# Six ring places up to the 78th gather, the second tile's projection and norm over slots 40 to 81, late modulation rows behind the attention output

## What is computed

```python
mod = silu(c) @ w_ada + b_ada                      # sh1 sc1 g1 sh2 sc2 g2, 6 x 1024
h = x * (1 + sc1) + sh1
qa, ka, va, qb, kb, vb = split(h @ w_in)           # 1024 x 3072
ya = rms_norm(moba_attention(qa, ka, va)); yb = rms_norm(dilated_attention(qb, kb, vb))
y = concat([ya, yb]) @ w_out
x = layer_norm(ALPHA * x + (1 + g1) * y, ln1_g, ln1_b)
h2 = x * (1 + sc2) + sh2
# peer_ffn: 8 heads; product keys pick 16 of 16384 experts for each token and head
s1, s2 = scores of q = h2 @ w_q_peer against sub_keys   # top 16 of each, top 16 of the sums -> e, g
f = sum over the 128 picked experts of gelu(h2 . u[e]) * g * v[e]
x = layer_norm(ALPHA * x + (1 + g2) * f, ln2_g, ln2_b)
```

## Time and profile before

| what | us |
|---|---|
| median of 3 runs | 816.12 (815.91 to 816.32) |
| the profiled execution | 814.11 |
| its span in the trace | 812.3 |
| PE busy | 683.8 |
| VectorE busy | 581.1 |
| ScalarE busy | 346.0 |
| POOL busy | 291.3 |
| DMA | 323.74 MB, mean 399 GB/s |

### The profile page before, as it was taken

One profiled execution on the slowest core, in us unless ns is written; L12 is line 12 of the kernel. 1 busy time (PEld: TensorE's weight loads), 2 busy tenths in 40 slices (PEclk: granted clock), 3 DMA queues, 4 the chain that ended last, 5 costly groups with the idle time before them and its releaser, 6 DMA issues.

```text
span 812.3 us, 7319 instructions
## 1 busy us (share of the span) xinstructions
PE 683.8 (84%) x1988; PEld 325.7 (40%) x1988; DVE 581.1 (72%) x1349; ACT 346.0 (43%) x994; POOL 291.3 (36%) x263
## 2 busy tenths in 40 slices
PE   8999978998999898787989777787878787877785
PEld 4887644554544364443333223222323222222221
DVE  5566968787777987777777878767676757675455
ACT  0013322685575644353545355434343535353333
POOL 1000000344444365554454433443434343434340
PEclk9999999999999999997979999999999999999999
DMA  9999995899999999999999999999999999999993
GB/s 301 379 402 413 416 419 200 356 349 420 392 395 419 422 421 420 421 422 421 420 422 422 419 422 422 420 421 422 422 422 420 422 422 421 422 421 422 421 411 137
DMA packets 57213, 323.74 MB, mean 399 GB/s; under 512 B 6162, under 2 KB 16722, under 8 KB 20946
## 3 DMA queue, kind: packets, MB, share of 16 engines
q0 software_dynamic: 37152, 268.45, 80.0%
q1 hardware_dynamic: 19138, 54.55, 17.5%
q10 hardware_dynamic: 882, 0.27, 0.2%
HBM read 322.18 MB, written 1.07 MB: 398 GB/s over the span
## 4 chain that ended last, share of the span: by engine, by line
DMA 55%; PE 23%; DVE 9%; ACT 6%; issue 4%; SPq 1%; POOL 1%; DVEq 0%; ACTq 0%
DMA ring<-in_experts,e_all 51%; PE bank L529 12%; PE bank L551 4%; DVE ring L882 4%; DMA QT_h2T<-in_w 2%; DMA ring<-in_w 2%; PE bank L601 2%; PE bank L518 2%; ACT diag L728 2%; DVE acc L1038 1%; ACT weight L719 1%; POOL ring L1203 1%; SPq L402 1%; ACT L715 1%; ACT gel L715 1%
## 5 line engine op out<-in xcount | busy, mean ns | idle before, releaser
L529 PE MATMUL bank<-ring,diag 128*128 128x512 f32 x956 | 473.1, 631 | 104.5 <-ACT diag L728 104.3
L1203 POOL DMA_INDIRECT ring<-in_experts,e_all x254 | 282.8, 1113 | 495.1 <-PE bank L529 301.5
L529 PEld LDWEIGHTS bank<-ring,diag 128*128 128x128 f32 x956 | 173.2, 196 | 380.7 <-ACT diag L728 225.8
L882 DVE CUSTOM_DVE_ANT_0 ring<-ring,T_h 128x1024 f32<-128x1024 f32 x128 | 156.7, 1225 | 109.1 <-DMA ring<-in_experts,e_all 109.1
L882 DVE CUSTOM_DVE_ANT_0 ring<-ring,h 128x1024 f32<-128x1024 f32 x128 | 156.6, 1224 | 63.7 <-DMA ring<-in_experts,e_all 61.2
L715 ACT ACTIVATE gel<-pre 128x1 f32<-128x1 f32 x256 | 51.8, 202 | 313.3 <-DVE pre L882 312.5
L728 ACT ACTIVATE diag<-consts,weight 128x128 f32<-128x128 f32 x239 | 95.9, 401 | 7.8
L719 ACT ACTIVATE weight<-gel,g_all 128x1 f32<-128x1 f32 x256 | 75.4, 295 | 9.3
L1038 DVE SCALAR_TENSOR_TENSOR acc<-ring,cact,acc 128x512 f32<-128x512 f32 x56 | 42.1, 752 | 5.4 <-DMA ring<-in_w 3.0
L551 PE MATMUL bank<-hT_yT,lnw 128*128 128x256 f32 x128 | 28.7, 380 | 0.9 <-DVE hT_yT L1003 0.9
L601 PE MATMUL bank<-ring,hT_yT 128*128 128x512 f32 x64 | 28.5, 596 | 0.7 <-DMA ring<-in_w 0.7
(11 more groups left out here) (195 smaller groups left out, 572.9 us busy)
## 6 DMA issues: line engine op xcount, KB each, us to landing
ring<-in_w SPq DMA_DIRECT2D x16, 1024.0 KB, 14.2
H_s<-in_w SPq DMA_DIRECT2D x7, 1024.0 KB, 10.1
ring<-in_w SPq DMA_DIRECT2D x12, 512.0 KB, 10.5
ring<-in_w SPq DMA_DIRECT2D x16, 256.0 KB, 6.5
lnw<-in_w SPq DMA_DIRECT2D x4, 1024.0 KB, 17.7
ring<-in_experts,e_all POOLq DMA_INDIRECT x254, 14.8
H_s<-in_w SPq DMA_DIRECT2D x5, 512.0 KB, 8.2
lnw<-in_w SPq DMA_DIRECT2D x4, 512.0 KB, 8.4
```

The lines of the kernel that those rows point to most:

```text
L529: last = nc.tensor.matmul(tile_sum(t)[n], diag[:, m % DIAGS, :], ring[:, RING_AT[i], D + CH * n:D + CH * n + CH], start=(s == 0), stop=(s ...
L882: nc.vector.tensor_tensor_reduce(ring[:, r, 0:D], ring[:, r, 0:D], h2[i // SLOTS], 1.0, 0.0, ALU.mult, ALU.add, pre[:, i % PAIR:i % PAIR + ...
L1203: nc.gpsimd.indirect_dma_start(ring[:, r, :], None, A["experts"], bass.IndirectOffsetOnAxis(ap=e_all[:, i:i + 1], axis=0)).then_inc(slot_i ...
```

## The change

`WIDE_FROM` goes from 42 to 78, so gathers 42 to 77 use six places. In `PLAN` the first two rows of chunk 10 (`wsuma`, 10, 0) stand behind `yT` (0, 1) and `wo` (0, 0, 1) and no longer ahead of `PV` 2 and 3. `BESIDE` is written anew: nothing but the copy of v is left at slot 0, the units of S come in pairs at 2, 10, 19 and 27, `wo` at 40, 41, 49 and 52, `xa` at 52, `ln1a` at 56, `ln1b` at 67, `hT` at 70, the queries of tile 1 at 72 to 81. Slots 38 and 45 are added by VectorE. Slot 11 comes two places behind its dot. `ln1b` writes `h2` in two halves, and each transpose waits for its own half.

```diff
--- before.py
+++ after.py
@@ -80,7 +80,7 @@
 
 NARROW = [0, 1, 6, 7, 4, 5]
 WIDE = [2, 3] + NARROW
-WIDE_FROM = 42
+WIDE_FROM = 78
 
 
 G1, SH2, SC2, G2 = range(4)
@@ -100,8 +100,8 @@
        ("wsum", 4), ("S", 0), ("S", 1), ("v", 0, 0), ("wsum", 5), ("qk", 2, 0), ("qk", 2, 1), ("Tr", 0), ("Tr", 1), ("PV", 0), ("PV", 1), ("modrow", 0), ("madd", 0),
        ("yT", 0, 0), ("wsum", 6), ("qk", 3, 0), ("modrow", 1), ("madd", 1), ("wsum", 7),
        ("qk", 3, 1), ("modrow", 2), ("madd", 2), ("wsum", 8), ("S", 2), ("S", 3), ("modrow", 3), ("madd", 3), ("wsum", 9), ("v", 1, 0),
-       ("modrow", 4), ("madd", 4), ("Tr", 2), ("Tr", 3), ("wsuma", 11), ("wo", 0, 0, 0), ("wsuma", 10, 0), ("PV", 2), ("PV", 3), ("ny", 0), ("modrow", 5), ("madd", 5),
-       ("yT", 0, 1), ("wo", 0, 0, 1), ("xa", 0), ("wsuma", 10, 1), ("wo", 0, 1, 0), ("rows2",), ("wo", 0, 1, 1), ("ln1a", 0),
+       ("modrow", 4), ("madd", 4), ("Tr", 2), ("Tr", 3), ("wsuma", 11), ("wo", 0, 0, 0), ("PV", 2), ("PV", 3), ("ny", 0), ("modrow", 5), ("madd", 5),
+       ("yT", 0, 1), ("wo", 0, 0, 1), ("wsuma", 10, 0), ("xa", 0), ("wsuma", 10, 1), ("wo", 0, 1, 0), ("rows2",), ("wo", 0, 1, 1), ("ln1a", 0),
        ("va", 1, 1), ("ln1b", 0), ("hT", 0, 0), ("hT", 0, 1), ("wsumb", 10), ("wsumb", 11), ("q", 0, 0),
        ("s", 0, 0, 0), ("s", 0, 0, 1), ("v", 1, 1), ("modrow", 6), ("madd", 6), ("modrow", 7)]
     + [("piece", 0, 0), ("early",), ("q", 0, 1)] + [("piece", 0, j) for j in range(1, EXP_PIECE)] + [("v", 0, 1)]
@@ -110,18 +110,18 @@
 
 HEAD1 = [(1,), (2, 3), (4,), (5, 6), (7,), (8,), (9, 10), (11,)]
 LAG = 2
-NARROW_LAG, NARROW_TO = 1, 12
+NARROW_LAG, NARROW_TO = 1, 11
 VA_STEPS = 6
 
-BY_DVE = [20, 22, 35, 36, 37] + [i for i in range(48, 112) if i % 16 in (2, 4, 5)]
+BY_DVE = [20, 22, 35, 36, 37, 38, 45] + [i for i in range(48, 112) if i % 16 in (2, 4, 5)]
 FOLD = 114
 BESIDE = {
-    0: [("vcopy", 0, 1), ("S", 4), ("S", 5), ("Tr", 4)], 2: [("PV", 4), ("Tr", 5)], 3: [("s", 0, 1, 0), ("s", 0, 1, 1)], 5: [("PV", 5)],
-    6: [("S", 6), ("S", 7)], 8: [("Tr", 6), ("Tr", 7)], 12: [("PV", 6)], 15: [("PV", 7), ("S", 8)], 17: [("S", 9)], 19: [("yT", 1, 1), ("Tr", 8)],
-    20: [("Tr", 9)], 23: [("PV", 8)], 25: [("PV", 9), ("S", 10), ("S", 11)], 27: [("q", 0, 2)], 28: [("Tr", 10)], 29: [("s", 0, 2, 0)], 32: [("Tr", 11)],
-    34: [("PV", 10), ("s", 0, 2, 1)], 36: [("PV", 11)], 37: [("ny", 1), ("yT", 1, 0)], 38: [("wo", 1, 1, 0), ("wo", 1, 0, 0)],
-    40: [("wo", 1, 1, 1), ("wo", 1, 0, 1), ("xa", 1)], 44: [("ln1a", 1)], 47: [("ln1b", 1)], 50: [("hT", 1, 0), ("hT", 1, 1)], 52: [("q", 1, 2)],
-    56: [("q", 0, 3)], 60: [("q", 1, 3)], 66: [("s", 0, 3, 0)], 68: [("q", 1, 0)], 70: [("s", 0, 3, 1)], 76: [("q", 1, 1)], 116: [("x1", 0)], 119: [("x1", 1)],
+    0: [("vcopy", 0, 1)], 2: [("S", 4), ("S", 5)], 3: [("Tr", 4)], 4: [("s", 0, 1, 0)], 5: [("s", 0, 1, 1)], 6: [("PV", 4), ("Tr", 5)],
+    10: [("PV", 5), ("S", 6), ("S", 7)], 13: [("Tr", 6), ("Tr", 7)], 16: [("PV", 6), ("PV", 7)], 19: [("S", 8), ("S", 9)], 21: [("yT", 1, 1), ("Tr", 8)],
+    22: [("Tr", 9)], 23: [("PV", 8)], 25: [("PV", 9)], 27: [("S", 10), ("S", 11)], 30: [("q", 0, 2)], 32: [("Tr", 10), ("s", 0, 2, 0)], 34: [("Tr", 11)],
+    35: [("PV", 10), ("PV", 11), ("ny", 1)], 38: [("yT", 1, 0)], 39: [("s", 0, 2, 1)], 40: [("wo", 1, 1, 0)], 41: [("wo", 1, 0, 0)], 43: [("q", 0, 3)],
+    49: [("wo", 1, 1, 1)], 52: [("wo", 1, 0, 1), ("xa", 1)], 56: [("ln1a", 1)], 66: [("s", 0, 3, 0)], 67: [("ln1b", 1)], 68: [("s", 0, 3, 1)],
+    70: [("hT", 1, 0), ("hT", 1, 1)], 72: [("q", 1, 2)], 75: [("q", 1, 3)], 78: [("q", 1, 0)], 81: [("q", 1, 1)], 116: [("x1", 0)], 119: [("x1", 1)],
 } | {84 + 2 * i + z: [("s", 1, i, z)] for i in range(4) for z in range(2)} | {96 + 2 * j: [("lnb", j // 2, j % 2)] for j in range(8)}
 
 
@@ -658,7 +658,7 @@
                     product(dst[:], lambda k: yT[t][:, KC // 2 * g + k, :], lambda k: w[:, KC // 2 * g + k, :], KC // 2).then_inc(full, 1)
                 elif kind == "hT":
                     t, i = step[1:]
-                    pe.wait_ge(h2_ready, t + 1)
+                    pe.wait_ge(h2_ready, 2 * t + i + 1)
                     for j in range(4):
                         last = nc.tensor.transpose(dst[:, P * j:P * j + P], h2[t][:, P * (4 * i + j):P * (4 * i + j) + P], ident)
                     last.then_inc(full, 1)
@@ -1120,8 +1120,10 @@
                     dve.wait_ge(rows2_ready, 1)
                     centre(t, x[:, t, :], mod[:, SC2, :], h2[t])
                     inverse(t)
-                    scale(t, h2[t], mod[:, SH2, :], h2[t]).then_inc(h2_ready, 1)
-                    dve.wait_ge(h2_ready, t + 1)
+                    for n in range(2):
+                        half = slice(CH * n, CH * n + CH)
+                        scale(t, h2[t][:, half], mod[:, SH2, half], h2[t][:, half]).then_inc(h2_ready, 1)
+                    dve.wait_ge(h2_ready, 2 * t + 2)
                 elif kind == "x1":
                     t = step[1]
                     filled(dve, ("PV", len(UNITS) - 1))
```

## The result

The changed kernel takes 822.61 us (median of 4 runs, 819.28 to 823.61) against 816.01 beside it (815.03 to 816.32): the ratio is 1.0079, interval 1.0051 to 1.0108, so it is slower by 6.6 us. The profiled execution is its fastest: 819.28 us with a span of 817.4, 5.1 more than the span before. What follows explains these 5.1 us; the 2 to 4 us by which the other runs are longer are in no trace.

What follows compares the result with a forecast made beforehand. The DMA's ceiling of about 420 GB/s bounds the kernel, so only its losses can change. Head -3.2, ring 1.3 + 4.7 = 6.0 against 7.5, so -1.5; together -4.7, from 816.12 to 811.4 us, range 806.3 to 816.5.

Steps and rivals of the forecast that it cites:

- The head: Way to the first gather: rows2 starts 2.9 us earlier, at ln1's landing, h2's halves give 0.3; 3.2 us gained.
- the 0.5 that was worked out: h2 in two halves in the head: PE starts its transposes 0.55 us earlier; 0.3 us was taken for the product.
- The start of the ring: Slot 0 right behind v(0,1): gather 6 at 153.0, and the 4.8 us lost there go but for about 0.5.
- up to slot 41: Ring from its start to slot 41: 1.3 us of loss in all, bounds 0.3 and 4, start's 0.5 included.
- Slots 42 to 77: Stretch now with six places: bursts of work bring holds over the limit; 4.7 us lost, bounds 0.5 and 13.
- limit of 8.7: Longest time in us from a gather's landing to the issue into its place that six places bear without loss.
- Slot 45: VectorE slot, added at 47 behind a long piece: hold 8.95 us, over the limit by 0.2.
- Slot 50: VectorE slot, added at 52 behind xa: hold 10.7 us, over the limit by 2.0.
- Slots 36 and 37: Among slots 35 to 38: holds reach 9.2 us, but SP's 1 MB load gives VectorE 2.5 us; no loss.
- Slot 70: Not priced by itself; PE's queries at 72 to 81 pile up 4 to 5 us, mostly meeting eight places: nothing.
- The clock: PE after idling runs near 1.2 GHz: up to 3.4 us for slot 57, elsewhere only in the bounds.
- The second rival, on the other side: Six places starve between 42 and 77, bursts delay gathers, idle PE returns at half rate: 821 us; chance 0.18.

Runs made afterwards that it cites:

- pe_only: The changed kernel with slots 45, 50, 52, 53, 66, 68 and 69 on PE and not on VectorE; 812.06 us.
- wide48: The changed kernel with WIDE_FROM = 48 in place of 78, so eight places from gather 48 on; 812.31 us.
- pe_60s: The changed kernel with slots 66, 68 and 69 on PE, while 45, 50, 52 and 53 stay on VectorE; 818.69 us.
- dve_lag1: The changed kernel, but a slot under 78 that VectorE adds is added one place behind its dot and not two; 816.48 us.
- head_only: The kernel before with two edits alone: the two rows of chunk 10 behind yT and wo, and h2 of ln1b in two halves; 812.33 us.

## Why the prediction was wrong

**The head: right in its step, 2.2 us in place of 3.2.** ln1's landing is what comes late next, as forecast, and rows2 starts 2.85 us earlier (122.44 to 119.59). The halves of h2 let the first transposes start 3.38 us earlier (132.56 to 129.18), so they gave the 0.5 that was worked out. But the work ahead of them had moved up by more than rows2, PE had idled for 4.15 us, and the transposes and the product run in part at the lower clock: the product starts 2.92 us earlier and ends 2.20 earlier. The forecast had no term for that.

**The start of the ring: right.** Slot 0 right behind v (0, 1), gather 6 at 153.96 where 153.0 was forecast, and 396 GB/s from 161 to 182 where the earlier trace rows had 325. The ring loses about 3.4 us up to 264 where the forecast had 1.3 up to slot 41, within its bounds of 0.3 and 4.

**Slots 42 to 77: the failed step.** The sum of 4.7 us was 11.0 in the trace (window 264 to 370), and with dents before 264 the dots from 41 to 89 took 12.1 us longer than their landings need. What failed is the price of a hold: so many us over a limit of 8.7, each slot by itself, and nothing below it. The lost time is that between dots that waited for their landings, less 2.49 us for each gather:

| slot | hold worked out | hold measured | forecast to cost | lost | seen at dots |
|---|---|---|---|---|---|
| 36, 37 | up to 9.2 | 10.5, 10.3 | nothing | 1.9 | 43 |
| 45 | 8.95 | 8.65 | 0.2 | 2.2 | 51 |
| 50 | 10.7 | 12.8 | 2.0 | 2.0 | 53 to 56 |
| 57 | 9.9 | about 9 | 1.2 | 1.5 | 63 |
| 66 | 10.0 | 9.7 | 1.3 | 2.2 | 68 to 73 |
| 70 | not given | about 11 | nothing | 1.4 | 76 |

Where the dot did not wait (57, 70) the landing is counted on from the one before, so the hold is an estimate. The places of four dents were named rightly; the sizes, and two whole terms, were not:
- The limit of 8.7 was too high. It was taken between slot 22 (9.1, loss) and slot 35 (8.6, no loss), and slot 35 was no fair test: SP's load of 1 MB, issued at 247.50, moved beside these gathers, and dot 38 stood 4.66 us behind dot 37. So gather 41 was still issued some 6 us ahead of the landing before it:

```profile
251.92 1.23 DVE L882 CUSTOM_DVE_ANT_0 ring<-ring,h 128x1024 f32<-128x1024 f32 x1 [1.16 <-DMA ring<-in_experts,e_all]
...
256.58 1.22 DVE L882 CUSTOM_DVE_ANT_0 ring<-ring,h 128x1024 f32<-128x1024 f32 x1 [1.63 <-DMA ring<-in_experts,e_all]
```

- Slot 45, "over by 0.2": its hold (268.59 to 277.24) was even a little shorter than worked out, and it cost 2.2 us (dot 50 to dot 51, 4.72 where a period is 2.49). POOL's issues stood 6.3 us apart, and gather 51 was issued only 3.8 us ahead of dot 50, which began with its landing. The price is not the part over a limit.
- Slot 50, "over by 2.0": the hold was 12.8 (281.09 to 293.93), not 10.7. It spans the landings of 51 and 52, and the dent at 51 came into it. A slot added by VectorE is lengthened by the starvation that the slots before it made; the sum took each by itself.
- Slots 36 and 37, "nothing": the forecast took SP's 1 MB for 2.5 us of slack. With that load, issued at 240.84 here, dot 38 waits 2.24 us for its landing (249.05), and slot 36's add stands behind that dot, at 250.80. The issues of gathers 42 and 43 at 252.35 and 254.69 are released by these adds.
- Slot 70 on PE behind the first query, "nothing": the query waited for ScalarE's copy of hT, which stands behind the weight of slot 70 and so behind slot 66's add and ln1b; PE idled 5.59 us.
- The clock was left "in the bounds, not in the sum elsewhere". PE's mean clock fell to 0.85 at 264 to 310; PE idles while VectorE has the slots, and what follows the idle time is slower. The Trainium skill's page "TensorE: Matmul & The Clock Gate", section "What's actually happening", has the throttled state as the default and activity as what releases it; pe_only's trace agrees, with more work on PE and a clock of 0.96. How much of pe_only's 10.9 us is clock and how much shorter holds was not taken apart. The clock alone does not make the valley: wide48 moves 419 GB/s there at 0.89.

The second rival, on the other side, had the mechanism, its sign and its point of decision right (a ring loss of 10.7; it was 14.4) and was given 0.18. Its price, 821, is what the kernel takes within 2 us, but that has luck in it: it supposed every hold 2 us longer, and only those of 36, 37 and 50 were longer at all among the slots that the forecast priced; the others cost more at holds no longer than worked out. What spoke for it and was read as a side remark was slot 22: a VectorE slot in six places with a hold of 9.1, in a stretch that lost 2.7 us.

## What to carry to other kernels

A buffer that is filled by an in-order queue is sized by the longest hold and not by the mean: before taking places from it, list the users that release late (here the adds that stand two landings behind their dot) and give those to the engine that releases soon, or place the bursts elsewhere. Take the limit from holds whose landings nothing else delayed. Price a stall by the trace's own stall and not by the excess over a threshold, and let one dent lengthen the next hold. When an edit bundles independent parts, ask of each alone: here two small ones were worth 3.4 us and the third lost them.

## What the runs showed that was not expected

- A late issue costs more than it seems: in the changed kernel a gap of 6.3 us between issues (270.93 to 277.24) cost 2.2 us, with the later gather issued 3.8 us ahead of the landing before it. In steps of 1 us the DMA moves 213 and 197 GB/s from 279 to 281 and 180 from 283 to 284, and is never idle for a whole step. Whether a queue that runs low is slow, or a gather needs time from its issue to its first bytes, no run took apart. For the second speaks gather 0, issued at 141.28: 25 GB/s from 142 to 143, 164 in the next step, 360 in the one after. The kernel before bore a gap of 5.7 us at 249.5 to 255.2 without loss; there the later gather was issued some 6 us ahead. That lead alone does not fix the loss: in pe_60s gather 76 was issued 3.9 us ahead and lost nothing.
- Taking work off PE made it slower: three slots took 8.49 us behind a wait of 4.99 us, and 5.3 to 5.4 without.
- The runs of one kernel lie 1.4 us apart (pe_60s, 4 runs) to 8.1 (dve_lag1, 10 runs). The changed kernel's 4.3 over 4 runs is no sign that starvation makes the spread: head_only, with eight places from gather 42 on, has 4.2 over 10 runs.
